# Gated DeltaNet chunks: the triangular system solved in two halves of 64 rows, in place of a joined 128-row inverse

## The reference

```
L = where(strict, (k * beta) @ k.T * decay, 0)        # strictly lower triangle, per head
sol = triangular_solve(L + eye, [v * beta, k * beta * exp(g)])
v_new = u - wk @ S                                    # u, wk: the two halves of sol
o = (q * exp(g)) @ S + where(tril, q @ k.T * decay, 0) @ v_new
S = S * exp(g_last) + (k * exp(g_last - g)).T @ v_new
```

## Time and profile before

| | |
|---|---|
| median of 3 runs | 1559.47 us (1558.28 to 1561.65) |
| profiled execution | 1563.35 us, span 1561.4 us |
| PE busy in the span | 1462.7 us, 94% |
| DVE, ACT, POOL busy | 900.3, 641.9, 222.0 us |
| DeltaNet recurrence | from 217 to 415 us of the span |
| PE busy from 217 to 415 us | 182.00 of 198.00 us |

### The profile page before, as it was taken

The page is one execution under the profiler, slowest core; times in us unless marked ns, Lnnn a source line. Parts: engine busy times, 40 slices in busy tenths (PEclk is TensorE's granted clock), DMA queues, the critical chain, the costliest instruction groups (busy, mean ns, idle before and its releaser), DMA issues. The chain is left out here.

```text
span 1561.4 us, 31581 instructions
## 1 busy us (share of the span) xinstructions
PE 1462.7 (94%) x13118; PEld 1299.0 (83%) x13118; DVE 900.3 (58%) x1198; ACT 641.9 (41%) x1079; POOL 222.0 (14%) x227
## 2 busy tenths in 40 slices
PE   6999989999899999999999997789789999999994
PEld 6999989897799999999999995459767767777772
DVE  5677545865655444344444844543466677676775
ACT  5343535441343222232334313643434565565661
POOL 0111026763130000000112000320001000000002
PEclk8999999999999999999999996889789999999997
DMA  6678240001523332322335430005148888888886
GB/s 180 228 260 279 98 107 18 2 3 56 173 69 97 96 92 81 107 72 74 93 92 151 116 110 1 1 1 161 69 138 274 277 281 295 283 298 268 272 285 236
DMA packets 169739, 226.10 MB, mean 145 GB/s; under 512 B 11272, under 2 KB 134689, under 8 KB 169545
## 3 DMA queue, kind: packets, MB, share of 16 engines
q1 hardware_dynamic: 160246, 191.44, 39.5%
q0 software_dynamic: 8512, 30.48, 5.5%
q10 hardware_dynamic: 862, 2.50, 0.5%
HBM read 188.78 MB, written 37.88 MB: 145 GB/s over the span
## 5 line engine op out<-in xcount | busy, mean ns | idle before, releaser
L276 DVE TENSOR_TENSOR w_lo<-w_raw,w_hi 128x2048 fp32r<-128x2048 f32 (+1 forms) x71 | 153.9, 2172 | 94.7 <-ACT w_hi L268 94.7
L268 ACT ACTIVATE w_hi<-w_raw 128x2048 fp32r<-128x2048 f32 (+1 forms) x71 | 128.1, 1810 | 124.6 <-PE P L221 115.3
L221 PE MATMUL P<-xf_hi,w_hi 128*128 128x260 f32 x704 | 141.9, 283 | 2.0 <-DVEq L1859 1.2
L221 PE MATMUL P<-xf_hi,w_lo 128*128 128x260 f32 x704 | 142.0, 283 | 0.0
L221 PE MATMUL P<-xf_lo,w_hi 128*128 128x260 f32 x704 | 141.8, 283 | 0.0
L221 PEld LDWEIGHTS P<-xf_hi,w_hi 128*128 128x128 f32 x704 | 108.5, 189 | 2.6 <-issue 1.4
L221 PEld LDWEIGHTS P<-xf_hi,w_lo 128*128 128x128 f32 x704 | 108.6, 189 | 0.0
L221 PEld LDWEIGHTS P<-xf_lo,w_hi 128*128 128x128 f32 x704 | 108.2, 188 | 0.0
L221 PE MATMUL P<-xa_hi,w_hi 128*128 128x260 f32 x512 | 104.2, 285 | 2.7 <-DVE xa_lo L319 2.7
L221 PE MATMUL P<-xa_lo,w_hi 128*128 128x260 f32 x512 | 104.0, 285 | 0.0
L221 PE MATMUL P<-xa_hi,w_lo 128*128 128x260 f32 x512 | 104.0, 285 | 0.0
(11 more groups left out here) (553 smaller groups left out, 3287.6 us busy)
## 6 DMA issues: line engine op xcount, KB each, us to landing
raw_more_moe<-in_moe_w_gu_dram SPq DMA_DIRECT2D x64, 512.0 KB, 5.4
w_raw<-in_moe_w_gu_dram SPq DMA_DIRECT2D x64, 512.0 KB, 5.5
w_raw<-in_dense_w_gu_dram SPq DMA_DIRECT2D x44, 512.0 KB, 5.0
expert_out<-zeros POOLq DMA_DIRECT2D x40, 512.0 KB, 4.1
w_raw<-in_a_w_in_dram SPq DMA_DIRECT2D x32, 512.0 KB, 5.1
raw_more_moe<-in_moe_w_down_dram SPq DMA_DIRECT2D x32, 512.0 KB, 5.0
w_raw<-in_moe_w_down_dram SPq DMA_DIRECT2D x32, 512.0 KB, 5.2
w_raw<-in_dense_w_down_dram SPq DMA_DIRECT2D x16, 384.0 KB, 3.9
```

Source lines behind the costliest of these rows:

```text
L221: ins = nc.tensor.matmul(out[:, b], w, x[:, b * HALF:(b + 1) * HALF], start=(first and n == 0), stop=(last and n == 2))
L268: ins = nc.scalar.activation(hi, raw, ACT.Copy)
L276: ins = nc.vector.tensor_tensor(lo, raw, hi.bitcast(F32), ALU.subtract)
```

## The change

The two inverses are no longer joined. The system is solved by forward substitution: W (the transposed inverse) of the upper block times the upper 64 rows of `VP` (`solve_upper`), ACT copies this out of PSUM into `WK` (`upper_values`), the corner times it (`carry`), DVE subtracts that from the lower 64 rows of `VP` (`less_carried`), and W of the lower block times these rows (`solve_lower`). All three products have 64 rows, 64 weight columns and 128 moving columns. `F` is gone, and its two buffers are a second buffer for `XW`, so that DVE's `first` of chunk n+1 no longer waits for the end of chunk n's joining.

```diff
+            def halved(rows, to, lhs, rhs):
+                for h in range(HL):
+                    ins = pe.matmul(to[rows[1], h], lhs[rows[0], h], rhs[rows[0], h], start=True, stop=True)
+                return ins
+
+            def solve_upper(g, n):
+                inv[g].after(pe, n, dve="XW32")
                 prep[g].after(pe, n, dve="VP")
                 if n:
                     chain[g].after(pe, n, dve="VS")
                 else:
                     pe.wait_ge(s_given, 1)
-                ins = full(bank(g, 2), big("F", g), big("VP", g, n))
+                ins = halved((upper, upper), bank(g, 2), W(g, n), big("VP", g, n))
...
+            def carry(g, n):
+                chain[g].after(pe, n, act="U1")
+                prep[g].after(pe, n, pool="LT12")
+                chain[g].done(halved((upper, lower), bank(g, 2), big("LT12", g, n), big("WK", g)), "pe", n, "LU")
+
+            def solve_lower(g, n):
+                chain[g].after(pe, n, dve="VL")
+                chain[g].done(halved((lower, lower), bank(g, 2), W(g, n), big("VP", g, n)), "pe", n, "U")
...
-                for g in both:
-                    join_one(g, n)
                 if more:
                     for g in both:
                         query_scores(g, n + 1)
...
                 for g in both:
-                    join_two(g, n)
+                    solve_upper(g, n)
                 if more:
                     for step in (first, values):
                         for g in both:
                             step(g, n + 1)
                 if last:
                     sample_outer(5)
-                    for g in both:
-                        last_from_state(g, n)
+                    last_from_state(0, n)
                 for g in both:
-                    solve(g, n)
-                if last:
-                    sample_outer(6)
+                    carry(g, n)
                 if more:
                     for g in both:
                         query_sums(g, n + 1)
+                if last:
+                    last_from_state(1, n)
+                for g in both:
+                    solve_lower(g, n)
+                if last:
+                    sample_outer(6)
...
-                for step in (corners, join, corner):
-                    for g in both:
-                        step(g, n)
+                for g in both:
+                    upper_values(g, n)
...
-                inv[g].after(dve, n - 1, pe="W64", act="F22")
-                inv[g].done(tt(W(g), for_heads(eye), E(g, 1), ALU.subtract), "dve", n, "W1")
+                chain[g].after(dve, n - 2, pe="U")
+                inv[g].done(tt(W(g, n), for_heads(eye), E(g, 1), ALU.subtract), "dve", n, "W1")
...
+            def less_carried(g, n):
+                chain[g].after(dve, n, pe="LU")
+                if n:
+                    chain[g].after(dve, n, dve="VS")
+                prep[g].after(dve, n, dve="VP")
+                VP = big("VP", g, n)
+                ins = tt(VP[lower], VP[lower], bank(g, 2)[lower], ALU.subtract)
```

More of the change, by code:

```diff
@@ L911, in _ @@
                         scale_corner(g, n + 1)
-            early.low(pool, lambda eng: inv[1].after(eng, NCH - 1, pe="W64", act="F22"))
+            early.low(pool, lambda eng: chain[1].after(eng, NCH - 1, pe="LU"))
         @block.tensor
@@ L986, in level_one @@
                     chain[g].after(pe, n - 1, dve="S")
-                inv[g].done(blocks(half(g, 0, 0), E(g, s), X(g)), "pe", n, f"Y{s}")
+                inv[g].done(blocks(half(g, 0, 0), E(g, s), X(g, n)), "pe", n, f"Y{s}")
             def level_two(g, n, s):
                 inv[g].after(pe, n, act=f"Y{s}")
[L991 to L1005, removed]
+                blocks(half(g, 1, 0), W(g, n), big("Y", g))
+                inv[g].done(blocks(half(g, 1, 1), big("Y", g), W(g, n)), "pe", n, f"XW{s}")
             def recall(g, n):
@@ L1245, in level, with upper_values @@
                 inv[g].done(copy(big("Y", g), half(g, 0, 0)), "act", n, f"Y{s}")
[L1247 to L1262, removed]
+            def upper_values(g, n):
+                chain[g].after(act, n, pe="U1")
+                prep[g].after(act, n + 1, act="sq_k")
+                chain[g].done(copy(big("WK", g)[upper], bank(g, 2)[upper]), "act", n, "U1")
             def square_out(g, n):
@@ L1352, in _ @@
                         sample_squares()
-                for step in (corners, join, corner):
-                    for g in both:
-                        step(g, n)
+                for g in both:
+                    upper_values(g, n)
                 if n == 0:
                     sample_roots()
-            early.high(act, lambda eng: inv[0].after(eng, NCH - 1, act="F22", pe="W64"))
+            early.high(act, lambda eng: chain[0].after(eng, NCH - 1, pe="LU"))
             for step in (square_out, root_out):
@@ L1430, in new_values @@
                 chain[g].after(dve, n - 1, pe="o_back")
[L1431 to L1435, removed]
+                chain[g].done(tt(big("VT", g), bank(g, 2), per_head(small("c", g, n)), ALU.mult), "dve", n, "v")
             def state_values(g, n):
@@ L1616, in _ @@
                             step(g, n + 1)
+                for g in both:
+                    less_carried(g, n)
                 if last:
@@ L3199, in decoder_step @@
                     bufs["S"] = [wide(front[:, g]), wide(own[g])]
[L3200 removed]
+                    bufs["XW"] = [piece.rearrange("p (a h x) -> p a h x", a=2, h=HL) for piece in (inverse[0], own[11 + g])]
                     bufs["LT12"] = halved(inverse[1])
```

36 lines of the change are left out of this document (17 added, 19 removed).

## The result

| | median (us) | runs | profiled execution (us) | its span (us) |
|---|---|---|---|---|
| before | 1560.14 | 4, 1558.28 to 1561.65 | 1563.35 | 1561.4 |
| changed | 1578.34 | 4, 1575.82 to 1581.17 | 1576.33 | 1574.6 |

The ratio is 1.0118, with a 95% interval of 1.0099 to 1.0137: slower, as forecast, but by 18 us and not by 10.7, which is outside the range. Two runs of the kernel before fell far outside (3073 and 6948 us); the ratios leave them out.

What follows compares the result with a forecast made beforehand. PE, busy for 94% of the span and without rest at chunk ends, was taken as the bound. 0.7 + 3.2 + 4.1 + 2.7 = +10.7 us on the median 1559.47 gave 1570.2 us, range 1563.5 to 1575.

Steps and rivals of the forecast that it cites:

- The price of the new products: Six halved PE groups at each chunk's end: 0.91 us a group, 5.5 us a chunk, PE's work up 1.6 us a chunk.
- the edge columns' row: PE's transpose with 11 weight and 128 moving columns: 0.110 us a record, so few weight columns save nothing against 128.
- The rival of half price: New products cost 0.52 us a group: +4.0 us in all, 1563.5 us; chance 0.14, shared with a middle price.
- The walks: Each chunk's end stepped forward on PE and DVE with their waits: delays of +0.7, +3.2, +4.1 and +2.7 us.
- POOL was not waiting for PE there: Level 16 of n = 1: POOL ends near 293.2 whatever PE does, so only +0.7 us is passed on from n = 0.
- the 2.26 us idle of level 16: PE's idle in n = 1 behind two tiny DVE operations beside POOL's; forecast to shrink below 1 us.
- n = 0's 2.0 us: Delay of `add_state` at the end of n = 0, 273.1 for 271.10; forecast as not all passed on.
- the clock takes more: Rival: one more half-clock stretch behind n = 0, or a longer one in `sample_scores`, each 2 to 4 us; chance 0.09.
- My own sign of being wrong: Prediction is wrong if groups are cheap, the recall's subtraction comes sooner, or clock stretches move by over 5 us together.
- My argument on the clock: Against the clock giving time back: thin query sums beside quarter-array groups, and added PE idling at recall and upper solve.
- PE idle of 0.47 us at the upper solve: Sign: PE idles 0.5 to 0.7 us for DVE ahead of the upper solve in n = 1 and 2.
- `sample_scores` held by "bq": End of n = 2: "bq" stands behind new values of group 1, so PE starts at 356.3 for 352.21, +4.1 us.

Runs made afterwards that it cites:

- thick sums: Query sums' moving side widened from 1 to 128 columns, in both kernels: changed 1573.32 us (ratio 1.0091), before 1559.12 us (0.9991).
- the paired one: Changed kernel without the carry, each head's upper and lower solve issued in turn, no solve behind the query sums: 1559.74 us, ratio 0.9994.

## Why the prediction was right in sign and wrong in size

**The price of the new products was right.** "I take 0.91 us a group": it measures 0.92, and the edge columns' row was the right neighbour. The rival of half price is false for this order; it is true of the same products when upper and lower halves alternate, 0.90 us for sixteen records. The Trainium skill (TensorE: Matmul & The Clock Gate, Why this matters for your kernels) says that a single matmul with 32 rows takes the time of one with 128, and that the gain is in tiles that run at once. The trace agrees for 64 rows, with 0.92 beside 0.90. The "up to 2x" of the Trainium skill (TensorEngine Tiling (Array Packing), Theoretical Speedup) came here only with the paired order.

**The walks, at full clock.** The two kernels with thick sums have little half-clock time, so their difference, from one same product of PE to the next, is the change's own price. The products are those on `G_tok` (behind `add_state`), the first of turning values back, `sample_scores` and the next phase's first:

| end of | forecast | changed | before | difference |
|---|---|---|---|---|
| n = 0, `G_tok` to `G_tok` | | 241.86 to 276.69 | 240.59 to 273.02 | +2.4 |
| and on, to turning back in n = 1 | +0.7 | to 301.92 | to 298.38 | -0.1 |
| n = 1, turning back to `G_tok` | +3.2 | to 320.99 | to 313.79 | +3.7 |
| and on, to turning back in n = 2 | | to 345.25 | to 338.05 | 0.0 |
| n = 2, to `sample_scores` | +4.1 | to 362.63 | to 350.85 | +4.6 |
| and on, to turning back in n = 3 | | to 399.77 | to 388.02 | 0.0 |
| n = 3, to the next phase | +2.7 | to 425.01 | to 410.33 | +2.9 |
| sum | +10.7 | | | +13.4 |

The recurrences differ by 1.1 us less (204.6 and 192.3), since this trace of before has one more half-clock stretch, ahead of the first `G_tok`.

**The step that failed: "POOL was not waiting for PE there".** I let the 2.26 us idle of level 16 take up 1.3 of n = 0's 2.0 us. It took up nothing: the idle is again 2.26 us in the changed kernel, and PE resumes at 298.16, 4.5 us after 293.69 (1.2 of them the later start of the phase, the rest the delay of n = 0 and the half-clock stretch at its end). POOL's timeline, then DVE's, of the changed kernel, ahead of it:

```profile
282.44 0.64 POOL L798 TENSOR_SCALAR_AFFINE_SELECT delta_own<-delta_own 128x512 f32<-128x512 f32 x1 [2.62 <-DVE delta_own L1354]
284.61 0.63 POOL L798 TENSOR_SCALAR_AFFINE_SELECT over_w_hi<-over_w_hi 128x512 f32<-128x512 f32 x1 [1.53 <-DVE over_w_hi L1354]
285.21 1.90 POOL L853 TENSOR_TENSOR s_state<-s_state,s_decay 128x1024 f32<-128x1024 f32 x1
...
293.66 3.74 POOL L853 TENSOR_TENSOR s_state<-s_state,s_decay 128x1024 f32<-128x1024 f32 x2
```

```profile
283.85 0.69 DVE L1354 TENSOR_TENSOR over_w_hi<-P,G_tok 128x512 f32<-128x512 f32 x1 [1.48 <-PE P L1038]
...
293.63 3.79 DVE L1450 SCALAR_TENSOR_TENSOR delta_small<-delta_small 128x4 f32<-128x4 f32 x2
```

The fades are queued behind the mask on POOL, the mask waits for DVE's difference of decays, and that waits for PE. POOL is late by what PE is late, one step removed. In the trace of before POOL already stood for 0.72 us ahead of the same mask (there DVE had copies of 2.23 us in front of its difference, and not a wait for PE):

```profile
279.53 0.63 POOL L802 TENSOR_SCALAR_AFFINE_SELECT delta_own<-delta_own 128x512 f32<-128x512 f32 x1 [0.72 <-DVE delta_own L1369]
```

I had looked at POOL's own queue at the place of the wait and not at what that queue stood behind. Worth 1.2 us of the miss.

**The walks themselves were 0.2 to 0.5 us short each.** In n = 1 the recall starts 305.45 - 302.85 = 2.60 us behind the query scores; I had 2.3. The upper solve starts at 5.09 us (I had 4.75) and `add_state` at 16.25 (I had 15.65). PE stands for 0.65 us at the recall, where my walk had 0.45: DVE takes up the query scores only at 304.60, 1.75 us behind PE's start of them, since its small operations stand before; I had 1.5. Together the walks miss about 1.5 us.

**The second step that failed, and the largest term: the clock.** My sum left the half-clock stretches of before where they were, so it put their change at nothing; "the clock takes more" was a rival with a chance of 0.09 and 2 to 4 us. The changed kernel has 23.8 us at 1.2 GHz in both of its traces, against 17.0 and 3.4 before. My own sign of being wrong, stretches that move by more than 5 us together, came true. Of the loss of 17 to 18 us, 13.4 are there at full clock (the medians with thick sums differ by 14.2), so 3 to 4 are the clock's; the thick sums, which take most of it out, give back 3.3 us in the changed kernel and 0.4 or nothing in the one before. That the clock is the cause of this part is shown by that one edit; the split between the terms is approximate, since a recurrence is known for one or two executions of each kernel.

My argument on the clock was half right: the new order does put thin sums beside products on one quarter of the array, and the stretches grew. That "less activity precedes these places" is not shown: PE worked without a pause for 6 us ahead of the one at n = 1. And I drew only a small chance from the argument. Whether it is the quarter-array products or only the thin ones that lower the clock stays open: in the kernel without a carry it stands at half as long as in the changed one, and the paired one has 17.0 us. That a gain of PE's own time brings less than its size is shown for the kernel without the carry (4 of 7.4 us) as idle time for DVE, with as much half-clock time as in the changed kernel; without the join (1.1 of 8 us) idle time explains 3 to 4 us, and the rest stays open.

**Right as forecast:** PE idle of 0.47 us at the upper solve; no waits for ACT's copy or the carried values; `sample_scores` held by "bq", with 0.94 us. Wrong: the next phase starts at 430.9 and not near 426, PE's idle at the recall of n = 2 is 1.05 us, and level 16's idle didn't shrink. From the end of turning back to the next level in n = 1 I had about 14 us: it is 14.4 with thick sums, and 16.1 in the changed kernel, part of it at half clock.

## What to carry to other kernels

Halving a triangular product saved nothing on PE where the halves followed each other: eight records of 64x64 cost the time of eight of 128x128 (0.92 and 0.90 us). It paid when two halves that don't depend on each other were issued in turn. Forward substitution makes them depend, with two results of DVE and ACT between them. Before counting on an idle gap to take up a delay, follow what the releasing engine's queue stands behind, back to the engine that you delay. And price a change of a PE-bound phase at full clock first, then look at whether thin products (one moving column) stand beside it: widening them cost 0.1 us a group at most here, and was worth 3.3 us in the changed kernel and nothing measurable in the one before.

## What the runs showed of the hardware that I had not expected

- The granted clock fell to 1.2 GHz while PE was busy without a gap (9.00 of 9.00 us at 0.62), behind products of one moving column. It did so much less when these had 128 columns, with the same number of instructions: 17.0 and 20.4 us at the ends of n = 0 to 2 became 0 and 3.4.
- One kernel's recurrence differs by 4.9 us between two executions (197.0 and 192.1, with 17.0 and 3.4 us at half clock): PE is busy for 182.0 and 176.2 us of it, and idle for 15.0 and 15.9.
- DVE operations of 128x4 that read two operands from SBUF last as long as POOL's operations of 128x1024 beside them (3.79 beside 3.75 us), and 0.22 us for two where the fades are gone. The Trainium skill (SBUF — State Buffer, "SBUF: two separate sides") describes an exclusive lock on the port pair that DVE and GpSimd share, held for a whole instruction, between a DVE operation with two SBUF inputs and a GpSimd one that reads SBUF. The traces agree: both conditions hold here, and with the fades moved away the 3.79 us are 0.22.
